# Moving the state's carry ahead of the read-out statistics, and four weight pieces one step forward, in the scan of a hybrid mLSTM block

## The reference

```python
m = jnp.maximum(jnp.maximum(s_loc.max(-1), s_ctx.max(-1)), sink_f)
e_loc = jnp.exp(s_loc - m[..., None])
...
out = (... e_loc ... vb + ... e_ctx ... vc) / den[..., None]
```

```python
C_new = decay[..., None, None] * C + jnp.einsum('bhs,bhsv,bhsk->bhvk', w, vc, kc)
n_new = decay[..., None] * nv + jnp.einsum('bhs,bhsk->bhk', w, kc)
...
num = jnp.einsum('bhts,bhsv->bhtv', s, vc) + inter[..., None] * jnp.einsum('bhtk,bhvk->bhtv', qc, C)
den = s.sum(-1) + inter * jnp.einsum('bhtk,bhk->bht', qc, nv)
h = num / jnp.maximum(jnp.abs(den), jnp.exp(-m_t))[..., None]
```

## Time and profile before

| what | value |
| --- | --- |
| median of 3 runs | 2253.76 us |
| the profiled execution's own time | 2253.94 us |
| its span, first to last instruction | 2252.2 us |
| mean granted TensorE clock | 0.989 |
| TensorE busy | 2203.1 us, 98% |
| VectorE busy | 1406.1 us, 62% |
| ScalarE busy | 859.9 us, 38% |
| GpSimd busy | 158.6 us, 7% |

### The profile page before, as it was taken

One profiled execution on the slowest core, in us unless ns is written; L12 is line 12 of the kernel. 1 busy time (PEld: TensorE's weight loads), 2 busy tenths in 40 slices (PEclk: granted clock), 3 DMA queues, 4 the chain that ended last, 5 costly groups with the idle time before them and its releaser, 6 DMA issues.

```text
span 2252.2 us, 31878 instructions
## 1 busy us (share of the span) xinstructions
PE 2203.1 (98%) x11991; PEld 1875.1 (83%) x11991; DVE 1406.1 (62%) x2365; ACT 859.9 (38%) x1477; POOL 158.6 (7%) x169
## 2 busy tenths in 40 slices
PE   9999999999999999999999999989999999999997
PEld 6888888888888888799778988878778888888886
DVE  5776685666446445644563255765777777767787
ACT  3622222222233424542344336751633232326444
POOL 0000000000000000045010002440000000000001
PEclk9999999999999999999999999999999999999999
DMA  7153344454265536423231001432334343438772
GB/s 282 44 158 113 108 117 126 145 152 141 69 246 172 185 119 195 122 66 114 69 111 39 19 20 47 132 99 64 115 115 142 110 147 109 148 120 312 277 234 103
DMA packets 237935, 293.08 MB, mean 130 GB/s; under 512 B 16694, under 2 KB 164846, under 8 KB 237806
## 3 DMA queue, kind: packets, MB, share of 16 engines
q1 hardware_dynamic: 226766, 282.81, 39.4%
q10 hardware_dynamic: 11040, 8.52, 1.2%
HBM read 233.48 MB, written 57.80 MB: 129 GB/s over the span
## 4 chain that ended last, share of the span: by engine, by line
PE 83%; DVE 7%; ACT 4%; DMA 3%; issue 2%; POOL 1%; SPq 0%; DVEq 0%; ACTq 0%; POOLq 0%
PE psum L1272 11%; PE psum L1273 11%; PE psum L1274 11%; PE psum L619 4%; PE psum L617 4%; PE psum L618 4%; PE psum L1439 2%; PE psum L2327 2%; PE psum L1440 2%; PE psum L1441 2%; PE psum L1910 2%; PE psum L1912 2%; PE psum L1911 2%; PE psum L2883 2%; DMA raw<-in_ffn_w 2%
## 5 line engine op out<-in xcount | busy, mean ns | idle before, releaser
L1272 PE MATMUL psum<-x_mix_h,x_op_h 128*128 128x512 f32 x640 | 249.9, 390 | 3.7 <-DVE v_sum L1090 3.7
L1273 PE MATMUL psum<-x_mix_l,x_op_h 128*128 128x512 f32 x640 | 249.5, 390 | 0.0
L1274 PE MATMUL psum<-x_mix_h,x_op_l 128*128 128x512 f32 x640 | 249.0, 389 | 0.0
L975 ACT ACTIVATE x_op_h<-raw 128x512 fp32r<-128x512 f32 x140 | 85.9, 627 | 209.3 <-PE psum L1274 127.0
L975 ACT ACTIVATE x_op_h<-w_sum 128x512 fp32r<-128x512 f32 x160 | 97.3, 624 | 158.0 <-DVE w_sum L953 92.9
L1272 PEld LDWEIGHTS psum<-x_mix_h,x_op_h 128*128 128x128 f32 x640 | 120.3, 188 | 28.6 <-DVE x_op_l L981 2.8
L1274 PEld LDWEIGHTS psum<-x_mix_h,x_op_l 128*128 128x128 f32 x640 | 120.2, 188 | 25.3
L1273 PEld LDWEIGHTS psum<-x_mix_l,x_op_h 128*128 128x128 f32 x640 | 120.3, 188 | 23.3
L1439 PE MATMUL psum<-s_high 128*128 128x512 f32 x308 | 120.4, 391 | 2.2 <-DVE s_low L1426 2.1
L1440 PE MATMUL psum<-s_low,s_high 128*128 128x512 f32 x308 | 119.9, 389 | 0.0
L1441 PE MATMUL psum<-s_high,s_low 128*128 128x512 f32 x308 | 119.8, 389 | 0.0
(11 more groups left out here) (410 smaller groups left out, 5705.3 us busy)
## 6 DMA issues: line engine op xcount, KB each, us to landing
raw<-in_ffn_w SPq DMA_DIRECT2D x154, 512.0 KB, 5.1
ada_slice<-in_w_ada SPq DMA_DIRECT2D x56, 512.0 KB, 3.8
f_terms<-g_half SPq DMA_DIRECT2D x77, 256.0 KB, 2.1
s_raw<-f_terms SPq DMA_DIRECT2D x77, 256.0 KB, 3.4
s_raw<-in_ffn_w SPq DMA_DIRECT2D x77, 256.0 KB, 4.1
f_rows<-g_out SPq DMA_DIRECT2D x44, 256.0 KB, 2.0
p_raw<-in_w_in SPq DMA_DIRECT2D x22, 512.0 KB, 5.6
early<-in_w_ada SPq DMA_DIRECT2D x16, 512.0 KB, 6.4
```

The costliest lines, as they stand in the source:

```text
L975: nc.scalar.activation(op_tiles(F, op)[0][:], OP_SOURCE[op], ACT.Copy).then_inc(F.hi, 1)
L1272: nc.tensor.matmul(o, wh[:, k], high(k), start=i < 4 and k == 0, stop=False, skip_group_check=i > 3)
L1273: nc.tensor.matmul(o, wh[:, k], low(k), start=False, stop=False, skip_group_check=i > 3)
L1274: last = nc.tensor.matmul(o, wl[:, k], high(k), start=False, stop=k == KH - 1, skip_group_check=i > 3)
```

## The change

In each iteration of VectorE's loop the carry moves ahead of the statistics, and the low part of a w_out piece, which stood ahead of the carry one step after its high part was made, now stands behind the carry in the same step: piece i in iteration i for i = 0 to 3, where it was piece i - 1 in iteration i for i = 1 to 4. No other engine's order changes, and no instruction is added or removed.

```diff
@@ -2846,11 +2846,12 @@
                     maximum_dve(dve, ATT_Q + i)
                 if i:
                     value_dve(dve, ATT_Q + i - 1)
-                    stats_of(i - 1)
-                if 0 < i <= 4:
-                    out_low(dve, WO_PIECE + i - 1)
                 if LAT0 + i in UPDATES:
                     carry(LAT0 + i)
+                if i:
+                    stats_of(i - 1)
+                if i < 4:
+                    out_low(dve, WO_PIECE + i)
             divide(LAST - 1)
             value_dve(dve, len(ATT) - 1)
             for u in range(4):
```

## The result

The changed kernel takes 2268.97 us in the median of 5 runs (2266.71 to 2274.76), the kernel before 2253.76 (5 runs beside them, 2250.01 to 2254.91). The ratio is 1.0079 with a 95% interval from 1.0062 to 1.0096, so it is slower by 14 to 22 us. The two medians are 15.2 us apart and the ratio stands for 17.8; the record has 38 executions of the changed kernel in all, with a median of 2270.2 us. The forecast was 2269.8 us. The profiled execution took 2271.54 us, its span 2269.7, against 2252.2 before.

What follows compares the result with a forecast made beforehand. TensorE was taken as busy nearly throughout, with VectorE and ScalarE in a closed loop in late steps. 12.3 us (pieces) plus 3.6 us (carry) on 2253.94 gave 2269.8 us, own range 2266 to 2273, wider range 2260 to 2278.

Steps and rivals of the forecast that it cites:

- the carry starts no sooner: Late steps: the carry waits for ScalarE, so moving it ahead of the statistics leaves its start 2.05 us after the exponential.
- Part 1: Steps 0 to 3: each moved low part waits for its own high part, closing a loop through ScalarE; +12.3 us.
- the turn: Steps 0 to 3: one round of the loop through division, exponential, high part and low part takes 8.77 us.
- One collision with GpSimd: Division 0: L2789 waits for GpSimd's product L2640; 1.2 us, counted once.
- rival A: Steps 0 to 3: the port catches the division in every turn, three more of 1.2 to 2.4 us; chance 0.2.
- Part 2, the loop: Steps 9 to 13: statistics behind the carry lengthen the loop from 5.41 to 6.96 us, four times; +6.2 us.
- Step 14: Ahead of its transposes: 0.65 us of statistics remain, while division 13's two small instructions escape GpSimd, -1.9 us.
- The clock: Step 14: TensorE's shorter wait doesn't bring the granted clock down; -1.4 us, with 0 as the other end.
- B: Divisions 9 to 12: GpSimd's power blocks the small instructions behind the statistics, +3.7 us, 2273.5 in all; chance 0.1.
- C: Late steps: statistics cost nothing because GpSimd or TensorE is the real bound; only +9.0 us, 2262.9; chance 0.1.
- D: Both moved pieces stay hidden and the stall of step 14 shrinks; faster, 2250.6 us; chance 0.04.
- E: Both moved pieces stay hidden and the stall of step 14 remains; no measurable change, 2253.9 us; chance 0.03.

Runs made afterwards that it cites:

- e2: Kernel before, with only the low part of piece i moved behind carry i, for i = 0 to 3; ratio to before 1.0046.
- e3: Kernel before, with the low part of piece i - 1 behind the carry of step i, its high part a step old; ratio to before 1.0012.
- e9: Changed kernel with each high part ahead of the step's exponential, pieces 2 and 3 in steps 3 and 4; ratio to before 1.0037.
- e1: Kernel before, with only the carry moved ahead of the statistics, low parts left in place; ratio to before 1.0014.
- e4: Changed kernel with ScalarE's high part of piece i ahead of exponential i, for i = 0 to 3; ratio to before 1.0079.
- e5: Kernel before, with the carry ahead of the statistics in step 13 alone; ratio to before 1.0001.
- e8: Changed kernel with small filler products on TensorE where it waits in steps 10 to 15; 2266.74 us, ratio to before 1.0062.
- e7: Changed kernel with the division's first three instructions made two, each reading PSUM and one SBUF operand; 2263.18 us, ratio to before 1.0047.
- e6: Kernel before, with the division's first three instructions made two, each reading PSUM and one SBUF operand; ratio to before 0.9977.

## Why the prediction was right

Point by point, on the profiled execution:

- **That neither edit is hidden, and the carry starts no sooner.** Right: the carry stands 2.05 us behind the exponential in both kernels.
- **Part 1.** Forecast 12.3 us, measured 11.2 (e2 alone: 10.4 timed, 11.5 in its scan). The loop is the one named, shown by e3 and e9, which take the wait out of it. The term that was too large is the turn: 8.4 us instead of 8.77, and nearly all of that is the way from the exponential to the copy of the probabilities, taken as 2.3 us and measured as 1.95. I had read it in a step where ScalarE was held up, and with a full duration where the next start comes 0.1 sooner. One collision with GpSimd came where it was put (L2789 takes 1.27 us, 1.1 more than free), and none in the other three turns: there GpSimd's product began 2.0, 1.15 and 2.1 us behind the start of the division, not 0.7, so rival A was further off than its chance of 0.2 made it. The prediction gave the clock no term here, though it said that TensorE would wait twice in a step. It fell in steps 1 and 3, at a price of about 0.15 us in the turn of 8.53.
- **Part 2, the loop.** Forecast +6.2 up to step 13, measured 17.2 - 11.3 = 5.9 (from the transposes of step 9, 11.3 us late, to those of step 13, 17.2). e1 gives 6.0 between exponentials 9 and 13.
- **Step 14.** Forecast -1.25, measured -1.4. Division 13 escaped by less than 0.1 us where 0.2 was estimated. That is thin but not chance: the product is queued behind two small ones that wait for the same statistics, and it escaped in e1, e4, e5, e8 and e9 as well.
- **The clock.** This term failed. I took it that the shorter wait leaves the clock up and wrote -1.4. In the profiled execution the clock fell all the same and for longer, and with division 15 caught it is +3.1 us from the transposes of step 14 on. In e1, e4 and e9, with the same wait, the clock stayed up, and even there this stretch is only 0.8 us shorter than before: in e1 GpSimd caught L2788 of division 14 (0.80 us), and the transposes of step 15 waited 2.09 us instead of 1.46. So -1.4 was too much at its good end, and the other end, put at 0, should have been a loss.
- **The sum.** The scan is +18.9 instead of +15.9 us: 1.1 less in part 1, 0.3 less in the late turns, 4.5 more in the clock's term. The median lies 2.6 us below the profiled execution and so close to the forecast. That closeness is partly luck: an overrated turn and a clock term of the wrong sign cancel in part, and the profiled execution was one with a low clock (0.987; only 7 of the 38 have one as low), so the median lies below it.
- **Rivals.** A and B (the port in every turn; the power as a blocker) did not happen, and what the port costs in all isn't separated: e7's trace is 8.1 us shorter, but 3.9 us of that came back in e1, e4 and e9 with the old division, by the clock, and one instruction of every division is gone too. C is ruled out by e1, D and E by the measurement.

## What to carry to other kernels

An instruction moved forward to get it out of the way may have to wait for its own producer, and in an in-order queue everything behind it waits too: before moving, write down what it waits for, loads included (e4), and what is queued behind it. Work that fills a wait is free where it stands and costs its full length (1.49 us a turn for 1.55 us of statistics) as soon as it is put behind the waiting instruction, once that instruction is on a loop between two engines. To take the port's stalls away, change operands rather than times: reading the sum where it lies, in PSUM, saved an instruction and all collisions (e6). And where TensorE will wait in new places, give the clock a term in each of them, with a loss as one end.

## What the runs showed of the hardware

- **The half clock comes and goes with the same waits.** TensorE waited 1.93 or 1.94 us ahead of the transposes of step 14 in the changed kernel, e5, e1, e4 and e9. The granted clock fell to half level behind it in the first two and stayed at 1.00 in the last three. In the changed kernel it then stayed at 0.50 for 10 us, though TensorE was busy all that time. Behind the longer wait of 3.33 or 3.34 us it was low for some 3 us in the kernel before and in e3, and for 6.6 us in e2. What decides it is open.
- **The scatter between executions goes with the clock.** Each execution's mean granted clock is on record. Of the changed kernel's 38, the six at 0.986 and 0.987 take 2271.5 to 2274.8 us, the ten at 0.989 2269.8 in the mean, the seven at 0.991 and 0.992 2264.3 to 2267.7; the slowest, 2284.2, is at 0.982. The 61 executions of the kernel before that were timed beside the experiments go from 2255.8 in the mean at 0.988 to 2249.5 at 0.992. The mean is over the whole kernel, so it doesn't say in which stage the clock fell.
- **A VectorE instruction with one SBUF input can be caught as well.** The statistics' last steps in step 14 of the changed kernel, beside GpSimd's product:

```profile
1493.83 1.27 POOL L2648 TENSOR_TENSOR d_rows<-scores,d_rows 128x512 f32<-128x512 f32 x1
...
1494.32 0.81 DVE L2822 TENSOR_SCALAR small<-small 128x4 f32<-128x4 f32 x1
```

  L2822 takes 0.81 us instead of 0.17 and ends with the product, to 0.03 us. The same happens in e1, e4, e5, e8 and e9 (0.80 to 0.82 us). The Trainium skill (SBUF — State Buffer, "Who interferes with whom") names tensor_scalar among the forms that can take the shared ports, and this row agrees.
- **GpSimd's small power does not block.** In four divisions of the changed kernel L2788 and L2789 ran inside it at 0.19 and 0.17 us. The products of 128 by 512 caught L2789 (1.27 and 1.19 us); the operation on 128 by 4 did so in no trace read here. The rule of the Trainium skill that was weighed in the prediction (SBUF — State Buffer, "Who interferes with whom") agrees with the first rows and not with the second, and there the measurement decides.
